# Four edits to a two-layer hybrid decoder step: the gates in pieces, probabilities by head, later cache loads, the result turned early

## Time and profile before

| | us |
|---|---|
| median of 3 timed runs (lowest to highest) | 1987.57 (1982.83 to 1990.75) |
| the profiled execution, its own time | 1989.41 |
| its span, first to last instruction | 1987.6 |
| TensorE busy | 1773.5 (89%) |
| VectorE busy | 850.0 (43%) |
| ScalarE busy | 608.0 (31%) |
| POOL busy | 589.1 (30%) |

### The profile page before, as it was taken

How to read it: one execution, slowest core, us unless ns; L and a number is a source line. 1 busy time by engine, 2 the same in 40 slices (tenths; PEclk the granted TensorE clock), 3 DMA queues, 4 the chain that set the end, 5 groups by cost and what they waited for, 6 DMA issues and landing times.

```text
span 1987.6 us, 31392 instructions
## 1 busy us (share of the span) xinstructions
PE 1773.5 (89%) x13456; PEld 1658.4 (83%) x13456; DVE 850.0 (43%) x1238; ACT 608.0 (31%) x1041; POOL 589.1 (30%) x260
## 2 busy tenths in 40 slices
PE   6799787987999999998999887866897899999997
PEld 5688555986899999998999856755886799999997
DVE  4666265534522111146847154669663442121211
ACT  3234202433433222232431211316333343231311
POOL 1222000430344444443443200001342044444432
PEclk9899666997999999999999976678998999999999
DMA  4131211370333333323332223014254033333332
GB/s 123 43 88 44 54 31 39 114 246 20 98 90 95 96 89 93 96 77 85 86 95 76 67 65 95 16 43 138 63 170 140 24 105 89 93 96 87 95 96 76
DMA packets 294044, 170.64 MB, mean 86 GB/s; under 512 B 18839, under 2 KB 281159, under 8 KB 293754
## 3 DMA queue, kind: packets, MB, share of 16 engines
q1 hardware_dynamic: 253016, 123.85, 22.5%
q10 hardware_dynamic: 40890, 44.79, 7.2%
HBM read 155.91 MB, written 13.84 MB: 85 GB/s over the span
## 4 chain that ended last, share of the span: by engine, by line
PE 77%; DVE 12%; ACT 3%; DMA 2%; issue 2%; ACTq 1%; POOL 0%; SPq 0%; DVEq 0%; POOLq 0%
PE banks L382 21%; PE banks L384 20%; PE banks L383 20%; DVE swa_s L1151 1%; PE banks L889 1%; PE banks L1798 1%; PE banks L732 1%; PE banks L1823 1%; PE banks L1839 1%; PE banks L2656 1%; DMA w_raw<-in_mem_wo 1%; PE banks L2535 1%; ACT w_hi L442 1%; PE banks L702 1%; DVE norm_acc L312 1%
## 5 line engine op out<-in xcount | busy, mean ns | idle before, releaser
L453 POOL TENSOR_TENSOR w_lo<-w_raw,w_hi 128x1024 fp32r<-128x1024 f32 (+2 forms) x256 | 588.9, 2301 | 1373.7 <-ACT w_hi L442 1373.5
L382 PE MATMUL banks<-xn_hi,w_hi 128*128 128x260 f32 (+1 forms) x1920 | 552.8, 288 | 10.6 <-issue 6.7
L384 PE MATMUL banks<-xn_hi,w_lo 128*128 128x260 f32 (+1 forms) x1920 | 544.8, 284 | 0.0
L383 PE MATMUL banks<-xn_lo,w_hi 128*128 128x260 f32 (+1 forms) x1920 | 543.1, 283 | 0.0
L442 ACT ACTIVATE w_hi<-w_raw 128x1024 fp32r<-128x1024 f32 (+2 forms) x256 | 252.8, 988 | 863.0 <-PE banks L384 810.6
L382 PEld LDWEIGHTS banks<-xn_hi,w_hi 128*128 128x128 f32 (+1 forms) x1920 | 360.6, 188 | 17.2 <-issue 11.1
L383 PEld LDWEIGHTS banks<-xn_lo,w_hi 128*128 128x128 f32 (+1 forms) x1920 | 360.4, 188 | 1.5
L384 PEld LDWEIGHTS banks<-xn_hi,w_lo 128*128 128x128 f32 (+1 forms) x1920 | 360.2, 188 | 0.7
L384 PE MATMUL banks<-hid_hi,w_lo 128*128 128x260 f32 x1024 | 289.4, 283 | 0.0
L382 PE MATMUL banks<-hid_hi,w_hi 128*128 128x260 f32 x1024 | 289.2, 282 | 0.0
L383 PE MATMUL banks<-hid_lo,w_hi 128*128 128x260 f32 x1024 | 288.4, 282 | 0.0
(11 more groups left out here) (483 smaller groups left out, 2679.7 us busy)
## 6 DMA issues: line engine op xcount, KB each, us to landing
w_raw<-in_ffn_w SPq DMA_DIRECT2D x128, 512.0 KB, 4.1
w_raw<-in_odd_w_in SPq DMA_DIRECT2D x36, 512.0 KB, 3.8
kc<-in_cache_mem_k ACTq DMA_DIRECT2D x16, 512.0 KB, 8.4
vc<-in_cache_mem_v ACTq DMA_DIRECT2D x16, 512.0 KB, 9.2
w_raw<-in_even_w_in SPq DMA_DIRECT2D x14, 512.0 KB, 3.7
w_raw<-in_odd_w_out SPq DMA_DIRECT2D x24, 256.0 KB, 2.8
w_raw<-in_mem_wk SPq DMA_DIRECT2D x8, 512.0 KB, 3.9
w_raw<-in_mem_wq SPq DMA_DIRECT2D x8, 512.0 KB, 3.8
```

The lines of the kernel that those rows point to most:

```text
L382: pe.matmul(out, hi[:, kk, 0:m], r, start=kk == 0, stop=False)
L383: pe.matmul(out, hi[:, kk, 0:m], q, start=False, stop=False)
L384: last = pe.matmul(out, lo[:, kk, 0:m], r, start=False, stop=kk == nk - 1)
L453: pool.tensor_tensor(k.w_lo[n % RING][:, view[0], view[1]], k.w_raw[n % RING][:, view[0], view[1]], k.w_hi[n % RING][:, view[0], view[1]]. ...
```

## The change

1. The gate steps are cut into six pieces, hung on tiles 2 to 7 and behind the norm and rope steps of these tiles: `dve_error` (subtract one, subtract), `dve_inverse` (reciprocal), `dve_log` (correct the logarithm, form the forget gate), `dve_running` (the scans), `dve_exponents`, `dve_carried` (the carried exponents). ScalarE's `act_exponents` moves from tile 3 to tile 7.
2. The sliding-window probabilities are divided head by head: four scalar operations with a pointer to the reciprocal instead of one tensor-tensor.
3. The loads of the cached values move from behind tile `first + 4` to behind `first + 7`, the last tile.
4. The last feed-forward gets no fence. Chunk c of the result is turned inside the tile that follows it (k step 4), copied by ScalarE behind that tile, and stored in two halves of the features. Only the last chunk is turned after the last tile.

Signals that nothing waits for are dropped as well (`relu_ready`, `ready`, `free` of `Center`).

```diff
@@ -984,12 +984,14 @@
     follow(tiles, 0, None, gates.act_load)
     follow(tiles, 0, gates.dve_input, gates.act_exp)
     follow(tiles, 1, gates.dve_one_plus, gates.act_log)
-    follow(tiles, 2, gates.dve_running)
-    follow(tiles, 3, gates.dve_exponents, gates.act_exponents)
     for t in tiles:
         t["pairs"] = 2
     qk = QueryKeyNorm(k, tiles, 1)
     qk.tile0 = len(k.tiles) + 1
+    for i, step in enumerate((gates.dve_error, gates.dve_inverse, gates.dve_log, gates.dve_running, gates.dve_exponents,
+                              gates.dve_carried)):
+        follow(tiles, 2 + i, step)
+    follow(tiles, 7, None, gates.act_exponents)
     even_turns(k, tiles, SwaPrompt(k, tiles, 8, qk.rope))
     for c in range(E_MO, E_MO + 4):
         def sigmoid(act, n, c=c):
@@ -1148,7 +1150,9 @@
         dve.wait_ge(self.exps.s, u + 1)
         k.dve_link(dve.tensor_tensor(r, self.den[u % 2][:, :], self.es[u % 2][:, :], ALU.add))
         k.dve_link(dve.reciprocal(r, r))
-        dve.tensor_tensor(s, s, r.unsqueeze(2).to_broadcast([P, 4, 2 * P]), ALU.mult).then_inc(self.probs.s, 1)
+        for h in range(4):
+            ins = dve.tensor_scalar(s[:, h, :], s[:, h, :], r[:, h:h + 1], None, ALU.mult)
+        ins.then_inc(self.probs.s, 1)
 
     def dve_out(self, dve, u):
         k, ps, c, cols = self.k, self.k.ps, 2 * (u % 2), slice(u // 2 * P, u // 2 * P + P)
@@ -1316,14 +1320,24 @@
         act.wait_ge(self.one_plus.s, self.nth)
         act.activation(self.l, self.u, ACT.Ln).then_inc(self.log.s, 1)
 
-    def dve_result(self, dve):
-        k, e, u, l, w = self.k, self.e, self.u, self.l, self.w
+    def dve_error(self, dve):
+        k, e, u, w = self.k, self.e, self.u, self.w
         dve.wait_ge(self.log.s, self.nth)
         k.dve_link(dve.tensor_scalar(w, u, -1.0, None, ALU.add))
         k.dve_link(dve.tensor_tensor(w, e, w, ALU.subtract))
-        k.dve_link(dve.reciprocal(u, u))
+
+    def dve_inverse(self, dve):
+        self.k.dve_link(dve.reciprocal(self.u, self.u))
+
+    def dve_corrected(self, dve):
+        k, u, l, w = self.k, self.u, self.l, self.w
         k.dve_link(dve.tensor_tensor(w, w, u, ALU.mult))
         k.dve_link(dve.tensor_tensor(l, l, w, ALU.add))
+
+    def dve_result(self, dve):
+        self.dve_error(dve)
+        self.dve_inverse(dve)
+        self.dve_corrected(dve)
 
 
 class EvenGates:
@@ -1337,7 +1351,7 @@
         (k.g_i, k.g_f, self.x, self.e, self.u, self.l, self.w, k.g_cum) = (
             k.big(f"gate_{n}", [4, TOK]) for n in ("i_", "f_", "x", "e", "u", "l", "w", "cum"))
         self.log1p = Log1pExp(k, self.x[:, :], self.e[:, :], self.u[:, :], self.l[:, :], self.w[:, :])
-        self.here, self.exponents, self.ready = (k.counter(f"gates_{n}") for n in ("m0_here", "exponents", "ready"))
+        self.here, self.exponents = (k.counter(f"gates_{n}") for n in ("m0_here", "exponents"))
 
     def act_load(self, act, n):
         act.dma_start(self.k.g_m0[:, :], self.k.A["state_mlstm_m"][0].rearrange("b h -> h b"),
@@ -1358,10 +1372,19 @@
     def act_log(self, act, n):
         self.log1p.act_log(act)
 
+    def dve_error(self, dve, n):
+        self.log1p.dve_error(dve)
+
+    def dve_inverse(self, dve, n):
+        self.log1p.dve_inverse(dve)
+
+    def dve_log(self, dve, n):
+        k = self.k
+        self.log1p.dve_corrected(dve)
+        k.dve_link(dve.scalar_tensor_tensor(k.g_f[:, :], self.x[:, :], 0.0, self.l[:, :], ALU.min, ALU.subtract))
+
     def dve_running(self, dve, n):
         k = self.k
-        self.log1p.dve_result(dve)
-        k.dve_link(dve.scalar_tensor_tensor(k.g_f[:, :], self.x[:, :], 0.0, self.l[:, :], ALU.min, ALU.subtract))
         k.dve_link(dve.memset(self.w[:, :], 0.0))
         for b in range(NBLK):
             c = slice(b * P, b * P + P)
@@ -1377,6 +1400,9 @@
         dve.tensor_tensor(k.g_ws[:, :], k.g_i[:, SEQ:TOK], k.g_m[:, SEQ:TOK], ALU.subtract)
         dve.tensor_tensor(k.g_c[:, 0:SEQ], k.g_i[:, 0:SEQ], k.g_cum[:, 0:SEQ], ALU.subtract)
         k.dve_link(dve.tensor_tensor(k.g_a[:, 0:SEQ], k.g_cum[:, 0:SEQ], k.g_m[:, 0:SEQ], ALU.subtract))
+
+    def dve_carried(self, dve, n):
+        k = self.k
         ins = dve.tensor_copy(k.g_cs[:, 0:P], k.g_a[:, 0:P])
         for b in range(1, NBLK):
             c = slice(b * P, b * P + P)
@@ -2138,7 +2164,7 @@
     m.vc = [k.big(f"vc{l}{b}", [P, 2, 512]) for b in range(8)]
     cross = Cross(k, m, l)
     follow(tiles, first, None, cross.load_keys)
-    follow(tiles, first + 4, None, cross.load_values)
+    follow(tiles, first + 7, None, cross.load_values)
     k.small.reset(2080 + 3 * TOK * 4)
     norm = NextNorm(k, V_XATT + DC * l, k.xc, (keys.rstd_ready, keys.base + 4))
     tiles[first]["normed"] = norm
@@ -2931,36 +2957,56 @@
             ffn.open_end = True
         normed = ffn.norm
         stages += mixed + crossed + [ffn]
-    return stages + [Emit(k)]
+    ffn.open_end = True
+    return stages + [Emit(k, ffn)]
 
 
 class Emit(Stage):
 
 
-    def __init__(self, k):
+
+    def __init__(self, k, ffn):
         super().__init__(k)
         k.big.reset()
         self.y = k.big("y_tok", [P, NBLK, D_MODEL])
+        k.big.reset(2 * DC * TOK * 4)
         self.ys = k.big("ys_tok", [NSAMPLE, D_MODEL])
-        items = []
+        self.turned, self.free = k.turn_signals
+        self.base = k.turn_count
+        k.turn_count += DC
+        self.tiles = len(k.tiles) - DC
+        mine = len(ffn.mine) - DC
+        for c in range(DC - 1):
+            ffn.mine[mine + c + 1][("pe_at", 4)] = [lambda pe, c=c: self.pe_turn(pe, c)]
+            follow(ffn.mine, mine + c + 1, None, lambda act, n, c=c: self.act_copy(act, c))
+
+    def pe_turn(self, pe, c):
+        k, ps = self.k, self.k.ps
+        pe.wait_ge(k.tile_out.s, self.tiles + c + 1)
+        if c:
+            pe.wait_ge(self.free.s, self.base + c)
         for n in range(NBLK):
-            for g in range(2):
-                items.append(([(k.x[:, 4 * g + c, n * P:n * P + P], c * P) for c in range(4)],
-                              lambda b: b[:, 0:512], self.y[:, n, 512 * g:512 * g + 512]))
-        for g in range(2):
-            items.append(([(k.x[:, 4 * g + c, SEQ:TOK], c * P) for c in range(4)],
-                          lambda b: b[0:8, 0:512], self.ys[:, 512 * g:512 * g + 512]))
-        self.turn = Turn(k, "emit", items)
-
-    def pe(self, pe): self.turn.pe(pe)
-    def dve(self, dve): self.turn.dve(dve)
+            pe.transpose(ps[:, 6, n * P:n * P + P], k.x[:, c, n * P:n * P + P], k.c("ident"))
+        at = c % 4 * P
+        pe.transpose(ps[0:8, 7, at:at + P], k.x[:, c, SEQ:TOK], k.c("ident")).then_inc(self.turned.s, 1)
+
+    def act_copy(self, act, c):
+        k, ps = self.k, self.k.ps
+        act.wait_ge(self.turned.s, self.base + c + 1)
+        if c % 4 == 3:
+            half = slice(512 * (c // 4), 512 * (c // 4) + 512)
+            act.activation(self.ys[:, half], ps[0:8, 7, :], ACT.Copy)
+        act.activation(self.y[:, :, c * P:c * P + P], blocks(ps[:, 6, :]), ACT.Copy).then_inc(self.free.s, 1)
+        if c % 4 == 3:
+            act.wait_ge(self.free.s, self.base + c + 1)
+            k.store(k.O["y_prompt"].rearrange("b (n p) d -> p (b n) d", p=P)[:, :, half], self.y[:, :, half])
+            k.store(k.O["y_sample"].rearrange("b t d -> (b t) d")[:, half], self.ys[:, half])
+
+    def pe(self, pe):
+        self.pe_turn(pe, DC - 1)
 
     def act(self, act):
-        k = self.k
-        self.turn.act(act)
-        act.wait_ge(self.turn.free.s, self.turn.base + len(self.turn.items))
-        k.store(k.O["y_prompt"].rearrange("b (n p) d -> p (b n) d", p=P), self.y[:, :, :])
-        k.store(k.O["y_sample"].rearrange("b t d -> (b t) d"), self.ys[:, :])
+        self.act_copy(act, DC - 1)
 
 
 def program(nc, A, C, O):
```

More of the change, by code:

```diff
@@ L780, in __init__ @@
         self.sqr = [k.small(f"sqr{layer}_{i}", [P, TOK]) for i in range(2)]
-        self.relu_ready, self.sq_ready, self.hid_ready = k.ffn_signals
+        self.sq_ready, self.hid_ready = k.ffn_signals
         self.hid0 = layer * FFN // P
@@ L2560, in __init__ @@
         self.chunks = chunks
-        self.mean, self.free = k.counter(f"{name}_mean"), k.counter(f"{name}_free")
+        self.mean = k.counter(f"{name}_mean")
     def act(self, act):
@@ L2988, in program @@
                                                       "probs", "p_turned", "pt", "pv", "o", "o_turned")]
-        k.ffn_signals = [k.counter(n) for n in ("relu_ready", "squared", "hidden_ready")]
+        k.ffn_signals = [k.counter(n) for n in ("squared", "hidden_ready")]
         stages = plan(k)
```

## The result

The changed kernel takes 1961.72 us (median of 4 runs, 1960.23 to 1966.25) against 1989.16 for the kernel before in the same session (1982.83 to 1992.07): a ratio of 0.9871, 95% interval 0.9852 to 0.9890, or 25.7 us less. Sent to the chip a second time, the same kernel gave 1963.71 and 0.9872 (0.9852 to 0.9892).

What follows compares the result with a forecast made beforehand. TensorE is busy for most of the span, so time is won only where it stands still or at the end. Gains 14.0 + 0 + 3.6 + 4.4 = 22.0 from the median 1987.57 give 1965.6 us, range 1955 to 1975.

Steps and rivals of the forecast that it cites:

- Gates: Tiles 2 to 7: six pieces remove 18.4 us of excess, less 4.1 for stalls and 0.3 charged; gain 14.0 us.
- the three stalls: Behind inverse, log and running: late copy, norm held by POOL, TensorE loses 1.4 us in each of three tiles.
- My list of the copies' moments: Sign for the gates: copies of tiles 2 to 7 at 49.4, 56.9, 64.4, 73.2, 82.1 and 90.0.
- The lower bound of 10.5: Gates' smallest gain, if each stall is twice as long and the first one also costs clock.
- the rival by which it would fall there: Stalls keep tiles 3 to 9 at the lower clock, up to 50 us more: about 1994 us; chance 0.03.
- the growing backlog: Rival: norm loses to POOL in every gate tile, 24 us of stalls, kernel about 1985 us; chance 0.04.
- Heads: Sliding-window probabilities: four scalar operations are held by POOL like the product they replace; gain 0.
- the rival of 4.7 us: Scalar heads not held: six sliding-window tiles fall from 9.94 to 9.16, 4.7 us more, 1960.9 us; chance 0.28.
- Values: Cached values issued last: weights 1.9 and 4.4 us sooner, issues cost 4.5; 1.8 gained, twice, 3.6 us.
- the price of the issues: Eight value issues on ScalarE's queue at the stage's end, ahead of its fence, charged at 4.5 us.
- End: Result turned in the last tiles: 8.1 + 7.6 before, less 4.1, 2.05 and 5.1; gain 4.4 us.
- The upper bound of 7: End's largest gain, if the transposes hide in the matmul stream and the store is 1 us quicker.

Runs made afterwards that it cites:

- alone: One part's hunks of the diff on the kernel before: gates 0.9937, heads 1.0004, values 0.9977, end 0.9973.
- the zeros earlier: Zeros of the running sum written two tiles of work earlier, on the kernel with later turn, gate pieces between norm and rope, and product: 1952.66 us, 0.9815.
- the last three runs: Zeros written earlier, with the product (0.9815); the same with heads in place of the product (0.9837); the changed kernel again (0.9872).

## Why the prediction was right

**Gates, 14.0 forecast, 13.7 in the profile, 12.5 alone.** The overruns, the late copies, the lost contest with POOL and the three stalls came as written. I had charged 1.4 a stall; the tiles were 1.57 longer. My list of the copies' moments left out an overrun that my text has: the copy forecast at 64.4 stood behind the inverse, 1.7 us too long, and came 9.05 us behind the one before it, not 7.5. The lower bound of 10.5 was also summed wrongly; its terms give less than 10. The clock is 1.00 in all of them, so the rival by which it would fall there is wrong, and so is the growing backlog: from tile 7 on nothing is late. (Against that rival I had put about 1 us of idle time in every sliding-window tile; the rows give 5.3 us over some nine tiles, about 0.6 each.) The rival's place was wrong as well: the clock fell, in one execution of two, in the first unit, for 3 us of work and not 50.

**Heads, 0 forecast, -2.8 in the profile, -1.3 in the second one, -0.8 (-3.6 to 2.0) alone.** This step failed in part. Right was that the scalar form is held like the product, 3.31 where 1.14 is free; the rival of 4.7 us is out. Wrong was to cost four instructions as one block. By the records each is held or not by itself, and POOL, which had waited for the product in the first unit, now gets in between the second and the third head. The three bounds that I gave (0.2 us a unit lost, 4.7 gained, 0) all lacked it: it costs 2.0 to 4.7 us once, depending on the clock behind it, and 0.15 a unit comes back since the last held part is shorter. The Trainium skill's page "SBUF — State Buffer", section "Who interferes with whom", calls the port pair of VectorE and GpSimd an exclusive lock that a scalar operation in a two-port mode wants too; the trace after agrees that a scalar operation is held (2.47 behind POOL where 0.35 is free); the mode it ran in no row names.

**Values, 3.6 forecast, 4.9 in the profile (2.2 and 2.7), 4.6 alone.** The mechanism was right: no wait for an output weight, the issues ahead of the scores. By the roundings the work behind the earlier weights came 5.9 us sooner in layer 0 and 6.6 in layer 1, where I had summed 1.9 + 4.4 = 6.3; the issues, which took 4.12 and 4.37 instead of 4.5, then gave back only 3.7 and 3.9 of it. So the price of the issues, charged in full at 4.5, is the term that was too high.

**End, 4.4 forecast, 4.9 to 5.1 in the profile, 5.4 alone.** The turned tiles cost 7 x 0.56 = 3.9 (4.1 forecast), the last turn to the store 1.9 (2.05), the store and what follows 5.0 (5.1): three terms, each 0.1 to 0.2 too high. The upper bound of 7 was summed wrongly; the terms named there give 9.5.

**The sum.** 22.0 forecast; the parts alone give 21.7, the four stretches of the profile 13.7 - 2.8 + 4.9 + 5.0 = 20.8. That these lie so close to 22.0 is partly luck: the heads' miss is made up in part by the values and the end, which gave more than forecast. The profile's other 8 us lie in stages that no edit touches: the mLSTM's clock, the mixers of layer 1, 2.0 us beside the loads of layer 1's cached keys, whose eight issues took 5.60 here, 6.26 before and 7.06 in the run with the gate pieces between norm and rope. That the forecast lies 4 us above the median is the part that is not explained.

**A faster version.** The turn one group later, the gate pieces between norm and rope and the product in place of heads give 1951.29 us, 0.9820 (0.9795 to 0.9844), and with the zeros earlier 1952.66, 0.9815 (0.9796 to 0.9835). That is 0.005 below the changed kernel; the intervals do not overlap, and in the session of the last three runs the medians are 1952.66 and 1963.71. The next thing in them is tile 6's norm, held for 2.69.

## What to carry to other kernels

Where two engines exclude each other, splitting one instruction into several gives the other engine a way in: count each piece as a contest of its own. When a held instruction makes TensorE wait, look first at where its consumer stands in the stream: moving the turn behind one more group of products won 4.8 to 6.2 us in the profiles, while changing the form of the held instruction won 0.15 us in each of six units. And put added work where an engine waits for another one's answer (between norm and rope), not behind it; but work that stands beside the competitor is held itself, so its undisturbed duration does not say when it ends.

## What the hardware showed that I had not expected

- A norm that by the records began 0.04 us ahead of POOL's instruction was held through it: 2.98 where 0.76 is undisturbed; one that began 0.40 ahead ran free and POOL took 2.60 instead of 2.38, and so did one that began 0.18 ahead (72.21 and 72.39 with the gate pieces between norm and rope; POOL took 2.82). But a scalar operation 0.03 ahead ran free in the kernel before (0.41 at 921.22), so at a few hundredths the records do not tell who is held. A head that began 0.24 ahead ran in 0.35, and the next, 0.02 behind, took 2.47.
- Scans over 4 partitions are held beside POOL like the wide instructions (3.55 where 1.36 is free), while the reciprocal of the same 4 rows took 3.38 both beside POOL (57.68, POOL at 57.41) and mostly clear of it (61.78).
- One program with the same 3.2 us wait of TensorE kept its clock in one execution and lost 1.3 us by its fall in another; single profiles of one kernel differ by several microseconds in stages that are the same.
